# 80 unused bytes behind every row of the h tiles

## The reference

```
def conv_ffn(x, w_gate, w_up, conv_w, conv_b, w_down):
    g = x @ w_gate                      # 256 x 2048 by 2048 x 5632
    u = x @ w_up
    gp = jnp.pad(g, ((0, 0), (CONV_WIDTH - 1, 0), (0, 0)))
    gc = conv_b
    for j in range(CONV_WIDTH):
        gc = gc + conv_w[j] * gp[:, j:j + S]
    return (jax.nn.silu(gc) * u) @ w_down   # h: 256 x 5632, by 5632 x 2048
```

## Time and profile before

| | us |
|---|---|
| median of three runs | 2224.53 |
| span of the profiled execution | 2222.5 |
| PE busy in it | 2208.0 (99%) |
| PE weight load busy | 1892.6 (85%) |
| DVE busy | 1397.8 (63%) |
| ACT busy | 1037.8 (47%) |
| POOL busy | 244.1 (11%) |

### The profile page before, as it was taken

One profiled execution on the slowest core, in us unless ns is written; L12 is line 12 of the kernel. 1 busy time (PEld: TensorE's weight loads), 2 busy tenths in 40 slices (PEclk: granted clock), 3 DMA queues, 4 the chain that ended last, 5 costly groups with the idle time before them and its releaser, 6 DMA issues.

```text
span 2222.5 us, 28282 instructions
## 1 busy us (share of the span) xinstructions
PE 2208.0 (99%) x11424; PEld 1892.6 (85%) x11424; DVE 1397.8 (63%) x1758; ACT 1037.8 (47%) x1295; POOL 244.1 (11%) x250
## 2 busy tenths in 40 slices
PE   9999999999999999999999999999999999999998
PEld 7888888888888888888888888888888888888886
DVE  6655576776667666544485566677766666664545
ACT  5444555444444444433454445554444444443343
POOL 1751000220000000000008410002200000000000
PEclk9999999999999999999999999999999999999999
DMA  8655565666666666666665555756666666666664
GB/s 278 194 167 160 157 215 174 189 190 190 190 190 189 190 189 205 219 192 193 190 190 170 162 162 150 225 173 189 189 190 189 190 189 190 189 211 215 191 195 155
DMA packets 214818, 420.92 MB, mean 189 GB/s; under 512 B 13056, under 2 KB 15136, under 8 KB 213664
## 3 DMA queue, kind: packets, MB, share of 16 engines
q1 hardware_dynamic: 211824, 406.37, 59.8%
q0 software_dynamic: 2432, 12.22, 1.6%
q10 hardware_dynamic: 432, 0.52, 0.1%
HBM read 416.97 MB, written 2.10 MB: 189 GB/s over the span
## 4 chain that ended last, share of the span: by engine, by line
PE 98%; DVE 1%; DMA 0%; ACT 0%; issue 0%; POOLq 0%; POOL 0%; SPq 0%; DVEq 0%
PE ps L1289 29%; PE ps L1177 16%; PE ps L1175 16%; PE ps L1176 16%; PE ps L1293 15%; PE ps L1220 1%; PE ps L1416 1%; PE ps L1390 1%; PE ps L1367 1%; DMA raw<-in_w_in_dram 0%; PE ps L1423 0%; PE ps L1163 0%; PE ps L1436 0%; PE ps L1437 0%; PE ps L1435 0%; PE ps L1454 0%
## 5 line engine op out<-in xcount | busy, mean ns | idle before, releaser
L820 DVE TENSOR_TENSOR wlo<-raw,whi 128x1024 fp32r<-128x1024 f32 x767 | 964.7, 1264 | 700.6 <-ACT whi L578 697.0
L578 ACT ACTIVATE whi<-raw 128x1024 fp32r<-128x1024 f32 x767 | 807.9, 1059 | 853.0 <-DMA raw<-in_w_down_dram 278.5
L1289 PE MATMUL ps<-xT,whi 128*128 128x512 f32 x2816 | 657.3, 390 | 0.0
L1289 PEld LDWEIGHTS ps<-xT,whi 128*128 128x128 f32 x2816 | 522.6, 188 | 104.3 <-ACT qkT L599 0.4
L1175 PE MATMUL ps<-whi,xT 128*128 128x512 f32 x920 | 369.0, 401 | 0.0
L1177 PE MATMUL ps<-whi,xT 128*128 128x512 f32 x920 | 359.3, 391 | 0.0
L1176 PE MATMUL ps<-wlo,xT 128*128 128x512 f32 x920 | 358.5, 390 | 0.0
L1293 PEld LDWEIGHTS ps<-xT,wlo 128*128 128x128 f32 x2816 | 350.6, 192 | 7.5
L1293 PE MATMUL ps<-xT,wlo 128*128 128x256 f32 x2816 | 352.9, 283 | 0.0
L1175 PE MATMUL ps<-whi,hT 128*128 128x512 f32 x696 | 270.9, 389 | 0.0
L1177 PE MATMUL ps<-whi,hT 128*128 128x512 f32 x696 | 270.9, 389 | 0.0
(11 more groups left out here) (203 smaller groups left out, 1203.5 us busy)
## 6 DMA issues: line engine op xcount, KB each, us to landing
raw<-in_w_gate_dram SPq DMA_DIRECT2D x176, 512.0 KB, 4.0
raw<-in_w_up_dram SPq DMA_DIRECT2D x176, 512.0 KB, 4.0
raw<-in_w_down_dram SPq DMA_DIRECT2D x176, 512.0 KB, 4.1
raw<-in_w_in_dram SPq DMA_DIRECT2D x175, 512.0 KB, 3.7
raw<-in_w_out_dram SPq DMA_DIRECT2D x64, 512.0 KB, 4.2
xres<-in_x_dram POOLq DMA_DIRECT2D x4, 512.0 KB, 5.7
lnb<-in_ln_g_dram POOLq DMA_DIRECT2D x2, 1024.0 KB, 7.5
lnb<-in_ln_b_dram POOLq DMA_DIRECT2D x2, 1024.0 KB, 10.4
```

Of the source, the lines that this page charges most:

```text
L578: act.activation(whi[:, s, :, :], raw[:, s, :, :], ACT.Copy).then_inc(hi_done, 1)
L820: dve.tensor_tensor(wlo[:, s, :, :], raw[:, s, :, :], whi[:, s, :, :].bitcast(F32), ALU.subtract)\
L1289: return pe.matmul(ps[:, bank, :], whi[:, s, kk, m * P:(m + 1) * P], xT[:, kt, :, :].rearrange("p a s -> p (a s)"), start=kt == 0, stop=kt ...
```

## The change

A row of the h tiles becomes 2 x 256 + 20 values long, 2128 bytes instead of 2048. The 20 values (80 bytes) behind the 512 used ones are neither written nor read. The view `hT` that all code uses keeps its shape [128, 44, 2, 256]; only the step between rows differs. The arena grows by 44 x 80 = 3520 bytes, and `lnb1`, which is placed from its end, starts 3520 bytes later.

```
+H_ROW = 2 * SEQ + 20
...
-        ctx.enter_context(nc.sbuf_tensor("arena", [P, (arena_base - here) // 4 + FT * 2 * SEQ], F32))
-        hT = nc.alloc_sbuf_tensor_at("hT", [P, FT, 2, SEQ], F32R, offset=arena_base)
+        ctx.enter_context(nc.sbuf_tensor("arena", [P, (arena_base - here) // 4 + FT * H_ROW], F32))
+        hT = nc.alloc_sbuf_tensor_at("hT", [P, FT, H_ROW], F32R, offset=arena_base)[:, :, 0:2 * SEQ]\
+            .rearrange("p f (a s) -> p f a s", a=2)
         lnb1 = nc.alloc_sbuf_tensor_at("lnb1", [P, 2, D_MODEL], F32,
-                                       offset=arena_base + FT * 2 * SEQ * 4 - 2 * D_MODEL * 4)
+                                       offset=arena_base + FT * H_ROW * 4 - 2 * D_MODEL * 4)
```

## The result

The changed kernel takes 2235.44 us (three runs, 2235.39 to 2235.69) against 2224.53 before: 10.9 us more, a ratio of 1.005 with a 95% interval of 1.0036 to 1.0063. It is slower, by little, but clear of the noise.

A forecast was written before the change was run, and what follows sets the result against it. The prediction took PE's own pace as the bound and every term of the change as 0: 2222.5 us of span plus 0, plus 2.0 us outside it, gives 2224.5 us, with an 8-in-10 range of 2217 to 2244 us.

The forecast's parts named there:

- What bounds the kernel: Whole kernel: PE's own pace sets the end, busy 2208.0 of 2222.5 us; the down projection holds no other wait.
- Each nanosecond there is 2.0 us of the end: Down projections: with no idle time, each nanosecond on the 1993 products with moved rows adds 2.0 us.
- (a) Load length: Weight loads in the down projections: 0.115 us to spare under 512 columns, 0.007 under 256; cost taken as 0.
- (b) Two operands disturbing each other: Load beside matmul in the down projections: within 0.0133 us a product either way, 26.5 us in all; taken as 0.
- the nearest rows: Mixer f32 products with operands at 128 and 256, showing no price for unequal starts; source of the 0 taken.
- The two statements of the Trainium skill: For PE: independent read ports mean unchanged time; the isolated-product formula gives 215.8 ns for 512 columns against 226.7 traced.
- a gain of up to 21.7 us: Down projections: 1993 products 10.9 ns shorter each, if equal starts caused the excess over the skill page's formula.
- The count: Down projections: 2088 x 42/44 = 1993 products of 512 columns have a moved row and could change pace.
- unequal starts delay the matmul: Rival, down projections: moved rows pay up to 0.0133 us a product; 13 us if half do, 2237.5 us; chance 0.27.
- The common start as the cost: Rival, down projections: equal starts cause the extra 0.0133 us, so spreading rows gives 2198 to 2219 us; chance 0.15.
- Slow loads: Rival, down projections: loads at twice their pace cost 5.0 us in the 48 256-column products, 2229.5 us; chance 0.06.
- Writers and lnb1: ACT and DVE writes of h rows: 0 to 0.05 us more each, hidden; lnb1's move: cost 0.

## Why the prediction was wrong

**What bounds the kernel: right.** The end moved with the sum of the distances between PE's starts, and with nothing else: 11.1 us in the down projections for 10.9 in the runs. "Each nanosecond there is 2.0 us of the end" held.

**(a) Load length: right.** The load's record stayed at 0.188 us, and the products of 256 columns, which have almost no cover, did not get slower. They got faster (0.1197 to 0.1184 us) while the long ones got slower, which no case of mine had.

**(b) Two operands disturbing each other: this step failed.** I bounded it by -0.0133 and +0.0133 us a product and took 0, "the value of the nearest rows". Those rows were f32 products of the mixer. They show no price for unequal starts, and it was wrong to carry that to the one-pass format: there the price is 0.0054 us on the mean of all rows, 0.0017 to 0.0071 by residue. They were also fewer than the text made them look. A call of an f32 matmul leaves two records in the trace, so the "two products" of L1442 are one call a layer, and the two cycles a column are those of one record, four for the call. The step even said that the trace has no such product, and the choice then hung on rows of another mode. The difference between the two formats was itself in the rows: 0.0133 us on top of the columns in the one, 0.005 in the other. That was a reason to hold them for different, and I used it only as an argument for a rival.

The two statements of the Trainium skill were weighed there. "SBUF — State Buffer", section "Who interferes with whom", gives PE two independent read ports. The traces here don't bear out what I took from it, that the addresses of the two can't matter to each other: a shift of the stationary operand against the moving one by 4 bytes costs 5.7 ns a product. The step from "TensorE: Matmul & The Clock Gate", section "Back-to-back issue gap", to a gain of up to 21.7 us fails too: no difference gave 512-column products a mean under 226.7 ns, where that section's formula has 215.8.

**The count.** I priced 1993 products, leaving out rows 0 and 32. The period is 256 bytes and not 512, so row 16, too, starts like its moving operand. All three are late nevertheless (0.2318 us for row 0, 0.2306 for row 16 and 0.2305 for row 32): a product's wait depends on what went before it. With 48 bytes between blocks the first products at 128 are late as well and the later ones are not (0.2267 us), and at +16 the delay can stay away altogether. How many products the delay lasts, and what sets it, I can't tell.

**The rivals.** The first one, unequal starts delay the matmul, was what happened. It was given 0.27 and priced 13 us from half of the full 0.0133; the measured share is 0.40 of it. The common start as the cost (0.15) is refuted by the table for 512 columns; for 256 the common start is the slowest of the places measured. Slow loads (0.06) did not occur.

**Writers and lnb1: right.** Both cost nothing: the writers' records stayed at 0.616 and 0.684 us, and lnb1's new place has its own kernel.

## What to carry to other kernels

Where PE runs one-pass fp32r products with 128 x 128 stationary operands back to back, as here, keep the start of the stationary operand equal to that of the moving one modulo 256 bytes for products of 512 columns, in whatever tile either lies. For products of 256 columns try the stationary operand 32 bytes below the moving one, the best of the differences measured for them. A padding is harmless if it is a multiple of 256 bytes. Such a cost shows in no wait and in no busy share (PE stands at 99% before and after), and only faintly in the modelled length of the matmul's record, so take the distance between two starts from the timeline first. And do not fill a gap in the evidence with rows of another number format.

## What the runs showed of the hardware

- The distance between one-pass products of 512 columns, in a long enough run of them, is 226.7 ns with equal starts modulo 256 and 228.3 to 233.8 ns with the other 16 differences tried, one of 4 bytes included (232.4). The exception is +16, which gave 226.7 ns right behind gate and up and 233.3 elsewhere.
- For 256 columns it is the other way: 119.7 ns with equal starts, 116.6 ns at a difference of -32, 118.5 at -80.
- The one shift of all tiles together that was tried, by 64 bytes, changes nothing: 2224.87 us.
- With unequal starts the distances follow a fixed pattern (229, 235, 231, 230, 235 ns for five products at +80). Why, why -64 and -16 are cheap, and which of PE's two reads waits, is open.
- An f32 matmul leaves two records for a call, with 0.430 us between the starts at 512 columns and 0.112 us at 128.
